# Up products: where in the on-chip memory the activations of the matmuls lie, and a copy of them for the second tile

## The reference, cut to what matters

```python
def conv_ffn(h, w_in, dw, w_out):
    u = causal_dwconv(h @ w_in, dw)          # w_in: 1024 x 5632
    gate, val = u[..., :D_FF], u[..., D_FF:]
    return (jax.nn.silu(gate) * val) @ w_out # w_out: 2816 x 1024

x = x + conv_ffn(rmsnorm(x, norm_ffn_g[layer]), ...)            # layers 0 and 1
a, val = jnp.split(rmsnorm_2(x, norm_ffn_g) @ w_up, 2, axis=-1)  # the third, in hybrid_layer
```

## Time and profile before

| | |
|---|---|
| median of three runs (lowest, highest) | 2608.09 us (2603.39, 2612.75) |
| profiled execution: its time, the span of its instructions | 2604.33 us, 2602.5 us |
| granted TensorE clock, mean | 0.986 of 2.4 GHz |
| busy share of the span: PE, PEld, DVE, ACT, POOL | 96%, 91%, 52%, 43%, 38% |
| of the chain that ended last | 83% on PE |

### The profile page before, as it was taken

The page is one execution under the profiler, slowest core; times in us unless marked ns, Lnnn a source line. Parts: engine busy times, 40 slices in busy tenths (PEclk is TensorE's granted clock), DMA queues, the critical chain, the costliest instruction groups (busy, mean ns, idle before and its releaser), DMA issues.

```text
span 2602.5 us, 62231 instructions
## 1 busy us (share of the span) xinstructions
PE 2506.9 (96%) x25266; PEld 2367.6 (91%) x25266; DVE 1340.9 (52%) x2035; ACT 1122.6 (43%) x1652; POOL 995.2 (38%) x488
## 2 busy tenths in 40 slices
PE   6999898999999999998999999999999999999998
PEld 6888796997999999977989999999998769999998
DVE  7657554613477741798533677612143344455521
ACT  7834455454444433334534344433244444444422
POOL 3324220461444444325322444444443104444442
PEclk8899999999999999999999999999999999999999
DMA  4221001251232233323212322233222103322232
GB/s 147 74 65 59 2 1 63 82 194 38 94 97 95 91 102 100 130 65 105 90 65 65 97 94 91 92 111 114 88 93 69 49 1 97 97 89 97 96 99 74
DMA packets 62180, 219.43 MB, mean 84 GB/s; under 512 B 6752, under 2 KB 9184, under 8 KB 61408
## 3 DMA queue, kind: packets, MB, share of 16 engines
q1 hardware_dynamic: 58880, 207.76, 24.4%
q10 hardware_dynamic: 3168, 9.75, 1.1%
HBM read 213.29 MB, written 4.19 MB: 84 GB/s over the span
## 4 chain that ended last, share of the span: by engine, by line
PE 83%; DVE 8%; issue 6%; ACT 2%; POOL 1%; DMA 0%; DVEq 0%; POOLq 0%; ACTq 0%
PE psum L571 70%; DVE psum L2698 5%; PE psum L713 3%; PE psum L721 2%; PE psum L1072 1%; PE psum L1021 1%; PE psum L1251 1%; POOL wl L520 1%; PE psum L1290 1%; DVE psum L2267 1%; PE psum L1253 0%; ACT wh L1382 0%; PE psum L683 0%; PE psum L1278 0%; PE psum L690 0%
## 5 line engine op out<-in xcount | busy, mean ns | idle before, releaser
L520 POOL TENSOR_TENSOR wl<-raw,wh 128x1024 fp32r<-128x1024 f32 x388 | 949.0, 2455 | 1464.0 <-ACT wh L1382 1463.6
L571 PE MATMUL psum<-acth,wh 128*128 128x256 f32 x3792 | 763.8, 283 | 20.6 <-DVE actl L2789 8.2
L571 PE MATMUL psum<-actl,wh 128*128 128x256 f32 x3792 | 753.9, 281 | 0.0
L571 PE MATMUL psum<-acth,wl 128*128 128x256 f32 x3792 | 753.3, 280 | 0.0
L1382 ACT ACTIVATE wh<-raw 128x1024 fp32r<-128x1024 f32 x388 | 407.1, 1056 | 625.1 <-PE psum L571 601.4
L571 PEld LDWEIGHTS psum<-acth,wh 128*128 128x128 f32 x3792 | 582.7, 189 | 38.1 <-issue 30.2
L571 PEld LDWEIGHTS psum<-acth,wl 128*128 128x128 f32 x3792 | 581.7, 189 | 0.0
L571 PEld LDWEIGHTS psum<-actl,wh 128*128 128x128 f32 x3792 | 581.5, 189 | 0.0
L2628 DVE TENSOR_TENSOR cu<-psum,rstd 128x512 f32<-128x512 f32 x132 | 91.1, 690 | 236.9 <-PE psum L571 219.6
L571 PE MATMUL psum<-hidh,wh 128*128 128x256 f32 x1056 | 210.0, 277 | 0.0
L571 PE MATMUL psum<-hidh,wl 128*128 128x256 f32 x1056 | 209.5, 277 | 0.0
(11 more groups left out here) (442 smaller groups left out, 4048.3 us busy)
## 6 DMA issues: line engine op xcount, KB each, us to landing
raw<-in_weights SPq DMA_DIRECT2D x388, 512.0 KB, 3.3
xt<-in_x SPq DMA_DIRECT2D x4, 512.0 KB, 5.4
xt<-in_x ACTq DMA_DIRECT2D x1, 2048.0 KB, 9.3
out_x<-xt SPq DMA_DIRECT2D x6, 256.0 KB, 2.3
mem<-in_mem ACTq DMA_DIRECT2D x1, 1024.0 KB, 11.0
memn<-memh ACTq DMA_DIRECT2D x1, 1024.0 KB, 7.0
memn<-meml ACTq DMA_DIRECT2D x1, 1024.0 KB, 10.0
memh<-memn ACTq DMA_DIRECT2D x1, 1024.0 KB, 4.7
```

The lines of the kernel that those rows point to most:

```text
L520: pool.tensor_tensor(wl[:, s, :], raw[:, s, :], wh[:, s, :].bitcast(F32), ALU.subtract).then_inc(split_done, 1)
L571: ins = pe.matmul(out[:, n:n + HALF], w, m[:, n:n + HALF], start=first and n == 0, stop=last and n + HALF >= out.shape[1])
```

## The change

It has four parts.

1. Two more names for memory that is there: `uph` and `upl`, 32 bytes behind `acth` and `actl`, at 67648 and 84032. These are 64 bytes beyond a multiple of 128 (and of 256). To make room, 32 bytes are added behind `actl`, `eps` becomes six columns of `par`, and `common` and `omu` move by 32 bytes; `tmp` and everything behind it stay.
2. `firsth` and `firstl` in `zone`, at 165088 and 181472, 96 bytes beyond a multiple of 128. The memory is unused there while they live.
3. In the stage before each `up`, the high and low parts go to `uph` and `upl`, and are also copied: ACT copies each block of `uph` into `firsth` behind the squares, and DVE each block of `upl` into `firstl` behind the sum of squares.
4. In `up` TensorE reads `uph` and `upl` for tile 0, then runs `norm_total`, waits for all the copies, reads `firsth` and `firstl` for tile 1, and reads `uph` and `upl` again for the 40 tiles of the loop (now tiles 2 to 41) and the two behind it.

```diff
         act_at = cursor[0]
         acth = place("acth", [P, KT, T], F32R)
         actl = place("actl", [P, KT, T], F32R)
-        par = place("par", [P, NPAR])
+        cursor[0] += 32
+        uph, upl = (at("up" + n, [P, KT, T], F32R, act_at + 32 + 16384 * j) for j, n in enumerate("hl"))
+        par = place("par", [P, NPAR + 6])
+        eps = par[:, NPAR:NPAR + 6]
         common = place("common", [P, 3 * P])
         omu = place("omu", [P, 7 * KT])
-        eps = place("eps", [P, 6])
...
+        firsth, firstl = (at("first" + n, [P, KT, T], F32R, zone + 49184 + 16384 * j) for j, n in enumerate("hl"))
+        assert act_at % 64 == 32 and zone % 128 == 64
...
             def ffn(l):
                 up, norm = f"up{l}", f"norm_ffn{l}"
-                tile(up, 0, norm, acth, actl)
+                tile(up, 0, norm, uph, upl)
                 norm_total(norm)
-                dense(up, norm, acth, actl, units=2 * FT - 4, skip=1)
-                for j in range(2 * FT - 3, 2 * FT):
-                    tile(up, j, norm, acth, actl)
+                pe.wait_ge(first_hi, KT * (l + 1))
+                pe.wait_ge(first_lo, KT * (l + 1))
+                tile(up, 1, norm, firsth, firstl)
+                dense(up, norm, uph, upl, units=2 * FT - 4, skip=2)
+                for j in range(2 * FT - 2, 2 * FT):
+                    tile(up, j, norm, uph, upl)
...
-            def deltas_normed(stage, per, norm, gain=None, h=acth):
+            def deltas_normed(stage, per, norm, gain=None, h=acth, again=None):
...
+                        if again:
+                            act.wait_ge(hi_ready, i * 4 + (g0 + s + 1))
+                            hold()
+                            act.activation(again[:, i * 4 + s, :], h[:, i * 4 + s, :].bitcast(F32),
+                                           ACT.Identity).then_inc(first_hi, 1)
...
-                deltas_normed(f"xo{l}", 1, f"norm_ffn{l}")
+                deltas_normed(f"xo{l}", 1, f"norm_ffn{l}", h=uph, again=firsth)
...
-                deltas_normed("out2", 1, "norm_ffn2")
+                deltas_normed("out2", 1, "norm_ffn2", h=uph, again=firsth)
...
+                        if again:
+                            dve.wait_ge(lo_ready, i * 4 + (g0 + s + 1 + SC))
+                            dve.tensor_copy(again[:, k, :], l[:, k, :].bitcast(F32)).then_inc(first_lo, 1)
...
-                residual_normed(f"xo{l}", 1, f"norm_ffn{l}", ["norm_ffn_g"], [rstd], l * KT)
+                residual_normed(f"xo{l}", 1, f"norm_ffn{l}", ["norm_ffn_g"], [rstd], l * KT, uph, upl, again=firstl)
...
-                residual_normed("out2", 1, "norm_ffn2", ["norm_ffn_g_2"], [rstd])
+                residual_normed("out2", 1, "norm_ffn2", ["norm_ffn_g_2"], [rstd], 0, uph, upl, again=firstl)
```

More of the change, by code:

```diff
@@ L428, in build_program @@
         mid_split = sem("mid_split")
+        first_hi, first_lo = sem("first_hi"), sem("first_lo")
         x_ready = sem("x_ready")
@@ L501, in _ @@
             sp.dma_start(common[:, :], dram["c_common"]).then_inc(common_in, 16)
-            sp.dma_start(par[:, :], dram["par"]).then_inc(par_in, 16)
+            sp.dma_start(par[:, 0:NPAR], dram["par"]).then_inc(par_in, 16)
             with sp.Fori(0, UNITS // SLOTS) as i:
@@ L2194, in residual, with residual_normed @@
                         added(stage, 1, skip, i, s)
-            def residual_normed(stage, per, norm, gain, acc, col=0, h=acth, l=actl, bias=None):
+            def residual_normed(stage, per, norm, gain, acc, col=0, h=acth, l=actl, bias=None, again=None):
                 x0, sq0, g0, n = plan(stage, "x"), plan(norm, "sq"), plan(norm, "split"), len(acc)
```

## The result

The changed kernel takes 2629.59 us (median of 4 runs, 2624.26 to 2632.67), the kernel before beside it 2607.86 (4 runs, 2603.39 to 2612.75). The ratio is 1.0087, with a 95% interval of 1.007 to 1.0104: slower by 22 us, where 20 us less had been forecast. The size is that of rival A, which had a chance of 0.04 in its full form.

A forecast was written before the change was run, and what follows sets the result against it. PE, busy 96% of the span, bounds the kernel. Faster tiles in three up stages give -20.1 us, all else counted as 0: 2608.1 - 20.1 = 2588 us, own range 2578.5 to 2594, up to 2601 with partial gains.

The forecast's parts named there:

- rival A: Up behind tile 1 and down run slow, after a pause or by remainder: +20 us, 2628; chance 0.06, full form 0.04.
- The 42 tiles: Tiles behind tile 1 in each of three up stages go from 5.600 to 5.440 us: -20.1 us in all.
- Tile 1: In up, reading firsth and firstl, it stays at 5.60 or 5.65 us: 0 to +0.05 a stage, taken as 0.
- tile 0: In up, it carries on the speed of the stage in front: sum -0.1 us, counted as 0.
- `down` keeps its speed: Down, entered fast from reads at 32 before, is now entered from fast reads at 64: 0.
- The copies: Eight on ACT and eight on DVE per stage before up, hidden: 0, upper end 0.9 us for DVE's.
- the supply: Weight splitting on POOL keeps up with the higher pace in up and into down0: 0.
- Rival B: Speeds belong to the stages and addresses don't matter: no gain, copies hidden, 2608; chance 0.04.
- The rule that the prediction quoted from the Trainium skill: Only crossing 16-byte lines costs, so the up tiles stay at 5.60 us and the time at 2608.

The follow-up runs named there:

- e2_first_32: Changed kernel with firsth and firstl 64 bytes further on, so tile 1 reads at 32 modulo 256: 2627.29 us, ratio 1.0059.
- e3_uph_192: Changed kernel with uph and upl 128 bytes further on, at 192 modulo 256, the copy for tile 1 still at 224: 2627.43 us, ratio 1.0058.
- e5_192_after_32: Changed kernel with uph and upl at 192 modulo 256 and the copy for tile 1 at 32: 2587.13 us, ratio 0.9933.
- e8_last_32: Changed kernel without copies, the last tile of each up stage reading 32 bytes lower, at 32 modulo 256: 2616.57 us, ratio 1.0048.
- e1_no_copy: Changed kernel without the copies and their wait, tile 1 reading uph and upl as well: 2630.44 us, ratio 1.0074.
- the scan: Kernel before, each up tile behind tile 0 reading at one of eight multiples of 32 within 256, all ordered pairs covered: 2616.28 us, one run.
- e10_all_192: Kernel before with the activations moved from 32 to 192 modulo 256 in every stage that reads them: 2617.62 us, ratio 1.0031.

## Why the prediction was wrong

*The 42 tiles* (-20.1 us): the step that failed. It held that reads at 64 beyond a multiple of 128, entered straight from an odd place, are fast. What the runs showed in its place: reads at 64 modulo 256 are slow (237.44 us for the 42 tiles, where 228.5 was forecast), and it takes 192 modulo 256, with the weights at a multiple of 256, and 32 in front to make them reliably fast. `uph` missed the first condition (`e2_first_32` stays slow with 32 in front), `firsth` the last (`e3_uph_192`), and of the four kernels with copies only the one that meets both is fast (`e5_192_after_32`). Every fast row lies at 192, and those of the earlier trace rows are entered from 32; the prediction reduced the addresses modulo 128, for which no row spoke. It named the difference in rival A and gave it 0.06 because "both entries of this kind that rows 2 and 4 show are fast"; these two entries were of one pair of places, 32 to 192, and so one observation. Taken as the unknown that it was, A would have deserved about the chance of the forecast, and the range an upper end beyond 2628.

*Tile 1* (0) and *tile 0* (0): together 12.30 us in `up0`, 12.07 before. Tile 0 behind a fast `headh` did not carry on its speed; at 64 it was slow behind fast and slow reads alike. Tile 1 was not at one of the two speeds that the prediction gave odd places: at 224 a block takes 0.710.

*`down` keeps its speed* (0): the rule held and its sign turned: it was entered slow. 124.37 - 119.69 = 4.7 us, three times 14. `e8_last_32` shows that it is inherited.

*The copies* (0 and 0) and *the supply* (0): right in size, by `e1_no_copy`. Of the bounds of 0.49 and 2.26 us for DVE's copy, the lower came: 0.42. But the path was not the one that the prediction told: the copy on ACT moved `wl` beside DVE's scaling in `up0` (1.95 us instead of 0.49), which left 0.4 us of the 1.5 before tile 1 and cost 0.1 us in tile 0. The path was not reckoned with, so that the size came out right is luck in that part.

*Rival A's sizes* were right: 2.1 and 4.6 us a stage forecast, 2.2 and 4.7 measured. But its condition was told as a pause or a remainder; it was the remainder, and without the copies and their wait (`e1_no_copy`) the loss is the same.

*Rival B* (no effect of addresses) is refuted: the scan has paces from 0.680 to 0.720 us by place. The rule that the prediction quoted from the Trainium skill ("SBUF — State Buffer", "Door 1: The DMA port swizzle") does not account for it: by lines of 16 bytes all eight places are equal.

## What to carry to other kernels

Before a number of a trace is turned into a rule on addresses, list the full remainder of every case seen, of the weights as well as of the activations, and count cases that share all of them as one. Where TensorE has no idle time, compare the distance between starts of equal matmuls over stages: 4% of the matmuls' time was to be had, or lost, through 64 bytes of one tile in 44. Up to 6% lay between the places of the scan. And read a stage's speed together with that of the stage in front: here two thirds of the loss fell into stages that the change doesn't touch, and in the trace of `e8_last_32` one tile at the right place gave it back.

## What the hardware showed that was not expected

A stream of these matmuls (128 x 256, new weights for every second one) has no single pace at the full clock. By its place it usually runs at 113.3 ns a matmul (192 when fast), 116.7 (32), 117.3 (160), 117.8 (64, and 192 when slow), 118.3 (224), 118.7 (128) or 120 (0 and 96), and with the weights moved by 64 bytes the two places then in use ran at 118.3 and 118.7, the paces of their distances from the weights. Which of its speeds comes is kept from tensor to tensor at 192 (30 of 30 passages), is nearly always made fast by a tensor at 32 in front (32 of 33), and is drawn anew behind small matmuls of another kind (`e10_all_192`, `up0` and `up2`).

This draw is probably a part of the scatter between runs, which no run shows by itself: `xo0` was slow before and fast after, and `e10_all_192`, whose activations lie at 192 in every stage, has a spread of 30 us over 10 runs, where `e5_192_after_32` has 4 over its four and the kernel before 16 over 14. What in the chip does this stays open. Nor was tried how weights at other places than 0 and 64 behave.
